# Delta-rule pairs of a hybrid two-layer trunk: causal mask in the exponent, no GpSimd products, sums of squares on column quarters, third scores ahead of the first turn

## The reference, cut to what matters

```python
q = l2norm(q) * (dk ** -0.5)
k = l2norm(k)                    # x * rsqrt(sum(x * x) + eps)
gdiff = gcum[..., :, None] - gcum[..., None, :]
decay = jnp.where(tri, jnp.exp(jnp.where(tri, gdiff, 0.0)), 0.0)
Lmat = jnp.where(strict, bc[..., :, None] * kk * decay, 0.0) + eye
sol = triangular_solve(Lmat, [v * beta, k * beta * exp(gcum)])   # u, w
qk = jnp.where(tri, einsum(qc, kc) * decay, 0.0)
q_dec = qc * jnp.exp(gcum)[..., None]
# per chunk: v_new = u - w @ state; o = q_dec @ state + qk @ v_new
#            state = state * g_last + k_dec^T @ v_new
o_a = rmsnorm(o_a, even_dn_norm) * silu(dn_gate)
```

## Time and profile before

| | |
|---|---|
| Median of 3 runs | 1393.7 us (1390.71 to 1393.97) |
| Profiled execution | 1391.1 us, span 1389.4 us |
| TensorE busy | 1334.3 us, 96% of the span |
| VectorE busy | 807.7 us, 58% |
| ScalarE busy | 576.4 us, 41% |
| GpSimd busy | 109.2 us, 8% |
| Mean granted TensorE clock | 0.98 of 2.4 GHz |

### The profile page before, as it was taken

The page is one execution under the profiler, slowest core; times in us unless marked ns, Lnnn a source line. Parts: engine busy times, 40 slices in busy tenths (PEclk is TensorE's granted clock), DMA queues, the critical chain, the costliest instruction groups (busy, mean ns, idle before and its releaser), DMA issues.

```text
span 1389.4 us, 21218 instructions
## 1 busy us (share of the span) xinstructions
PE 1334.3 (96%) x7859; PEld 1079.1 (78%) x7859; DVE 807.7 (58%) x1236; ACT 576.4 (41%) x800; POOL 109.2 (8%) x131
## 2 busy tenths in 40 slices
PE   7989989999999999999999999999999999999996
PEld 5878767777778888888888777777878888888885
DVE  4877765676656564355555655554756563455543
ACT  5522422464444442233344555554434542233342
POOL 1010010110221000000012001000310000000011
PEclk9999999999999999999999999999999999999998
DMA  8312012123345523433224322322324323433132
GB/s 256 97 33 62 16 33 61 47 61 121 92 117 157 136 81 91 113 91 104 74 79 121 106 59 76 103 75 75 91 63 116 93 68 110 124 91 91 57 94 61
DMA packets 218667, 124.95 MB, mean 90 GB/s; under 512 B 6063, under 2 KB 215450, under 8 KB 218356
## 3 DMA queue, kind: packets, MB, share of 16 engines
q1 hardware_dynamic: 213760, 112.52, 28.8%
q0 software_dynamic: 3664, 11.58, 2.9%
q10 hardware_dynamic: 1188, 0.08, 0.1%
HBM read 119.92 MB, written 9.48 MB: 93 GB/s over the span
## 4 chain that ended last, share of the span: by engine, by line
PE 87%; DVE 6%; ACT 3%; issue 2%; DMA 1%; SPq 0%; POOL 0%; DVEq 0%; ACTq 0%; POOLq 0%
PE acc L705 73%; PE acc L1159 3%; PE R L1028 2%; PE R L1042 2%; PE R L1132 1%; PE R L727 1%; DVE cta L1727 1%; PE R L837 1%; ACT wh L427 1%; PE R L884 1%; DMA xin<-in_x 1%; PE R L1091 1%; DVE wl L431 1%; DMA out<-ob 1%; DVE ml L1653 0%
## 5 line engine op out<-in xcount | busy, mean ns | idle before, releaser
L705 PE MATMUL acc<-mh,wh 128*128 128x512 f32 x1120 | 318.6, 405 | 3.2 <-ACT wh L1322 2.4
L705 PE MATMUL acc<-ml,wh 128*128 128x512 f32 x1120 | 313.0, 397 | 3.1 <-DVE ml L1653 3.1
L705 PE MATMUL acc<-mh,wl 128*128 128x512 f32 x1120 | 310.1, 396 | 1.3 <-DVE wl L1736 1.3
L431 DVE TENSOR_TENSOR wl<-raw,wh 128x2048 fp32r<-128x2048 f32 (+1 forms) x103 | 222.1, 2156 | 119.9 <-ACT wh L427 119.9
L427 ACT ACTIVATE wh<-raw 128x2048 fp32r<-128x2048 f32 (+1 forms) x111 | 200.6, 1808 | 135.6 <-PE acc L705 135.5
L705 PEld LDWEIGHTS acc<-mh,wh 128*128 128x128 f32 x1120 | 207.7, 190 | 56.2 <-issue 10.4
L705 PEld LDWEIGHTS acc<-ml,wh 128*128 128x128 f32 x1120 | 211.6, 191 | 50.8 <-DVE ml L1653 4.6
L705 PEld LDWEIGHTS acc<-mh,wl 128*128 128x128 f32 x1120 | 212.1, 191 | 47.4 <-DVE wl L1736 2.2
L2217 DVE SCALAR_TENSOR_TENSOR cta<-cb,pv,cta 128x512 f32<-128x512 f32 x88 | 66.1, 752 | 74.8 <-ACT cta L1591 68.4
L576 POOL TENSOR_TENSOR ssum<-ssum,sq 128x512 f32<-128x512 f32 x32 | 49.8, 1556 | 733.4 <-ACT sq L1272 732.7
L705 PE MATMUL acc<-ah,wl 128*128 128x512 f32 x352 | 95.4, 389 | 0.0
(11 more groups left out here) (321 smaller groups left out, 1481.9 us busy)
## 6 DMA issues: line engine op xcount, KB each, us to landing
raw<-in_ffn_w_in SPq DMA_DIRECT2D x88, 512.0 KB, 5.0
raw<-in_ffn_w_out SPq DMA_DIRECT2D x32, 384.0 KB, 4.0
raw<-in_even_w_in SPq DMA_DIRECT2D x23, 512.0 KB, 5.1
raw<-in_ffn_w_out SPq DMA_DIRECT2D x32, 320.0 KB, 3.6
raw<-in_odd_w_qkv SPq DMA_DIRECT2D x16, 512.0 KB, 4.9
rel_bias_extended<-rel_bias_rows POOLq DMA_DIRECT2D x16, 320.0 KB, 3.9
raw<-in_even_w_out SPq DMA_DIRECT2D x8, 512.0 KB, 4.8
raw<-in_odd_w_qkv SPq DMA_DIRECT2D x16, 256.0 KB, 3.1
```

What stands on the lines that cost most here:

```text
L431: nc.vector.tensor_tensor(wl[s][:, 0:n], raw[s][:, 0:n], wh[s][:, 0:n].bitcast(F32), ALU.subtract).then_inc(sem(f"w_tail{s}"), 1)
L705: last = nc.tensor.matmul(acc[2 * s + t][:, :], ws[0 if form[0] else 1][:, t, k, :], mov[0 if form[1] else 1][:, k, :], start=form == HEAD ...
```

## The change

The causal mask goes into the exponent of the transposed decay: VectorE adds a constant of 0 or -1e30 (C_CAUSAL) after the minimum with 0, so that the exponential is zero above the diagonal, and the product of qkD with the triangle is gone. The product of qd and qh moves from GpSimd to VectorE, into key_evac. token_sums uses column quarters: for each block of 128 tokens four products with 32 weight columns each, at four column positions of the array. In pair 1 the post-norm of pair 0 and the spread of q's norms come later, the transposes of v come behind Y64, key_evac and the copies of v stand elsewhere in VectorE's order, and some small buffers lie in other places. The tables of units and pieces are changed. In the attention heads the second scores come ahead of the transposes of v, in the odd pairs the third scores ahead of the first turn. Four masks are no longer in the constants.

```diff
-    put(C_M16, (row // 16 == col // 16) & (col < row))
-    for n, w in ((C_M32, 32), (C_M64, 64), (C_M128, 128)):
-        put(n, (row // w == col // w) & (row // (w // 2) > col // (w // 2)))
+    put(C_CAUSAL, np.where(row <= col, 0.0, NEG))
...
-                             ("u", "E64"), ("sqo", "A2"), ("os", "A2t")):
+                             ("u", "E64"), ("sqo", "A2"), ("os", "At")):
...
# GpSimd, dn_pair
-                for h in (0, 1):
-                    e = d[h]
-                    read(pool, ph, f"rq{h}", 0)
-                    read(pool, ph, f"grow{h}", 0)
-                    pool.tensor_tensor(e["qd"], e["qd"], e["qh"], ALU.mult).then_inc(sem(f"qd{h}"), 1)
-                for h in (0, 1):
-                    e = d[h]
-                    read(pool, ph, f"qk{h}", 0)
-                    pool.tensor_tensor(blk(e["qkD"]), blk(e["qkD"]), rows(triu), ALU.mult).then_inc(sem(f"qkD{h}"), 1)
-
             pool.wait_ge(sem("conv"), 12 * NH)
-            pool.wait_ge(sem("qkD1"), NH // 2)
+            read(pool, f"dn{NH // 2 - 1}", "qk1", 0)
...
# TensorE
                 for b in range(NB):
-                    last = nc.tensor.matmul(r[:, c0 + b:c0 + b + 1], squares[:, b * P:(b + 1) * P], ones[:, 0:1],
-                                            start=True, stop=True)
+                    for q in quarter:
+                        last = nc.tensor.matmul(r[q, c0 + b:c0 + b + 1], squares[:, b * P + q.start:b * P + q.stop],
+                                                ones[:, 0:1], start=True, stop=True, tile_position=(0, q.start))
...
                 give(fill, g[0])
+                spread(p, "rk", "sqk", "dk", p)
                 if p:
                     post_sums(p - 1)
-                spread(p, "rk", "sqk", "dk", p)
                 give(fill, g[1])
-                if p:
-                    post_rows(p - 1)
                 step(g[2], "kk", "kh", "kh", ["rk"])
-                spread(p, "rq", "sqq", "dq", p)
+                if p == 0:
+                    spread(p, "rq", "sqq", "dq", p)
...
-                g = ((4, 2, 4, 3, 3, 2, 1, 2, 2, 2, 2, 3, 2, 2), (2, 2, 2, 2, 2, 2, 1, 2, 1, 1, 1, 1, 1, 1))[p]
+                g = ((4, 2, 4, 3, 3, 2, 1, 1, 1, 1, 3, 3, 4, 3), (2, 2, 2, 2, 2, 2, 1, 2, 1, 1, 1, 1, 1, 1))[p]
                 pe.wait_ge(sem("small_U0"), p + 1)
                 tiles("c2", (0, "At", "A"), (2 * P, "A", "At"))
                 give(fill, g[0])
+                if p:
+                    post_rows(p - 1)
+                    spread(p, "rq", "sqq", "dq", p)
...
                 give(fill, g[5])
-                pe.wait_ge(sem("silu"), TURN[2 * p + 1, 2] + 1)
-                step(g[6], "vtok", "vT", None, ["ktok"])
...
                 give(fill, g[10])
+                pe.wait_ge(sem("silu"), TURN[2 * p + 1, 2] + 1)
+                step(g[6], "vtok", "vT", None, ["ktok"])
...
# diff_head
+                scores(ph, 0, 1, i)
                 values(ph, 0, UNIT["diff"] + i, vf)
-                scores(ph, 0, 1, i)
...
# odd_pair
                 values(ph, i, i + UNIT[ph], o_vf)
+                scores(ph, i, 2, i + NH)
                 turned(0)
-                scores(ph, i, 2, i + NH)
...
# ScalarE, dn_pair
-                n = ((2, 1, 0, 1, 2, 3, 1, 2), (2, 1, 0, 1, 1, 1, 1, 9))[p]
+                n = ((0, 3, 0, 0, 3, 1, 3, 2), (0, 1, 2, 0, 1, 2, 1, 9))[p]
...
# VectorE, dn_pair
-                    V.tensor_scalar(e["decT"], e["decT"], 0.0, None, ALU.min).then_inc(sem(f"dm{h}"), 1)
+                    V.scalar_tensor_tensor(out=blk(e["decT"]), in0=blk(e["decT"]), scalar=0.0, in1=rows(cblk(C_CAUSAL)),
+                                           op0=ALU.min, op1=ALU.add).then_inc(sem(f"dm{h}"), 1)
...
-                if p:
-                    post_inverse(p - 1)
+                piece("dk")
...
                 if p:
-                    post_out(p - 1)
+                    post_inverse(p - 1)
                 piece("kh")
...
                 V.tensor_tensor(eight(small["E"]), eight(small["N"]), each_eight(C_L32), ALU.mult)\
                     .then_inc(sem("small_E"), 1)
+                if p:
+                    post_out(p - 1)
...
                     V.tensor_tensor(blk(e["kd"]), blk(r[:, :]), cols(eg[h][:, 2 * NB:]), ALU.mult)
+                    read(dve, ph, f"rq{h}", 0)
+                    read(dve, ph, f"grow{h}", 0)
+                    V.tensor_tensor(e["qd"], e["qd"], e["qh"], ALU.mult).then_inc(sem(f"qd{h}"), 1)
...
                 small_update("cU1", None)
-                key_evac(0)
                 small_update("cU2", "cU1")
-                key_evac(1)
                 small_update("cU3", "cU2")
                 read(dve, ph, "cU3", 0)
                 V.transpose(small["T"], small["U"]).then_inc(sem("small_T"), 1)
-                for h in (0, 1):
-                    r = full(dve, ph, f"vtok{h}", 0)
-                    free(V.tensor_tensor(blk(d[h]["vb"]), blk(r[:, :]), cols(beta(h)), ALU.mult), ph, f"vtok{h}", 0)
+                key_evac(0)
...
                 piece("X32")
+                key_evac(1)
                 r = full(dve, ph, "Y64", 0)
                 free(V.tensor_copy(Y64, r[low, :]), ph, "Y64", 0)
+                for h in (0, 1):
+                    r = full(dve, ph, f"vtok{h}", 0)
+                    free(V.tensor_tensor(blk(d[h]["vb"]), blk(r[:, :]), cols(beta(h)), ALU.mult), ph, f"vtok{h}", 0)
...
             dn_pair(0, evacs,
-                    {"decays": 2, "kh": 1, "qh": 1, "qk": 1, "N": 2, "cU1": 1, "cU2": 1, "cU3": 1, "cX": 1, "Y32": 1, "X32": 1, "Y64": 1, "X64": 1, "vtok": 1, 0: 1, 1: 1, "o": 2})
+                    {"decays": 2, "kh": 1, "qh": 1, "qk": 1, "N": 1, "cU1": 1, "cU2": 1, "cU3": 2, "Y32": 1, "Y64": 1, "X64": 2, "vtok": 2, 0: 1, 1: 1, "o": 2})
             dn_pair(1, evacs,
-                    {"decays": 4, "kh": 1, "qh": 1, "qk": 1, "N": 2, "cU1": 1, "cU2": 1, "cU3": 1, "X32": 1, "X64": 1, 0: 1, "o": 9})
+                    {"decays": 4, "qh": 2, "qk": 1, "cU1": 1, "cU2": 1, "cU3": 2, "X32": 0, "Y64": 1, "X64": 2, 0: 1, "o": 9})
```

More of the change, by code:

```diff
@@ L60 @@
 PV_NORM = (PV_EVEN, PV_FFN, PV_ODD, PV_FFN + 8, PV_FIN)
-C_ID, C_ONE, C_TRIU, C_M16, C_M32, C_M64, C_M128, C_PERM = range(8)
-C_COS, C_SIN, C_MASK = 8 * P, 8 * P + S, 8 * P + 2 * S
-C_I32, C_L16, C_L32 = [8 * P + 3 * S + 32 * n for n in range(3)]
-C_WIDTH = 8 * P + 3 * S + 96
+C_ID, C_ONE, C_TRIU, C_CAUSAL, C_PERM = range(5)
+C_COS, C_SIN, C_MASK = 5 * P, 5 * P + S, 5 * P + 2 * S
+C_I32, C_L16, C_L32 = [5 * P + 3 * S + 32 * n for n in range(3)]
+C_WIDTH = 5 * P + 3 * S + 96
 def constants():
@@ L300, in build @@
         for n, where, at in (("A", d[0]["A"], 0), ("At", d[0]["A"], 1), ("N", d[1]["A"], 0), ("E", d[1]["A"], 1),
-                             ("A2", d[0]["A2"], 0), ("A2t", d[0]["A2"], 1), ("A4", d[0]["A2t"], 0),
-                             ("A4t", d[0]["A2t"], 1), ("A8", d[1]["A2"], 0), ("T", d[1]["A2"], 1), ("U", d[1]["A2t"], 0),
+                             ("A2", d[0]["sqk"], 0), ("A2t", d[0]["sqk"], 1), ("A4", d[0]["A2t"], 0),
+                             ("A4t", d[0]["A2t"], 1), ("A8", d[1]["sqk"], 0), ("T", d[1]["sqk"], 1), ("U", d[1]["A2t"], 0),
                              ("Y", d[1]["A2t"], 1), ("Y32", d[0]["A"], 0)):
@@ L1003, in dn_pair @@
                             pe.wait_ge(sem(f"qd{h}"), p + 1)
-                            pe.wait_ge(sem(f"qkD{h}"), p + 1)
+                            read(pe, ph, f"qk{h}", 0)
                         last = nc.tensor.matmul(o[h][:, t], vn[h][:, :], e["qkD"][:, t], start=(b == 0), stop=True)
@@ L1421, in pieces @@
                         next(evac, 0)
-                n = ((2, 1, 0, 1, 2, 3, 1, 2), (2, 1, 0, 1, 1, 1, 1, 9))[p]
+                n = ((0, 3, 0, 0, 3, 1, 3, 2), (0, 1, 2, 0, 1, 2, 1, 9))[p]
                 pieces(n[0])
-                small_out("c2", d[0]["A2"], n[1])
+                small_out("c2", d[0]["sqk"], n[1])
                 small_out("c4", d[0]["A2t"], n[2])
```

## The result

The changed kernel takes 1357.2 us (median of 4 runs) against 1392.3 us for the kernel before in the same session. One of the four, at 1476.2 us, was disturbed at a mean granted clock of 0.84 and is left out of everything that follows; the other three lie between 1356.1 and 1357.8 us, with a median of 1356.5, 35.7 us less than before. The ratio is 0.9745, 95% interval 0.9725 to 0.9765. The profiled execution took 1356.5 us (span 1354.7), 34.6 us less than that of before.

The account below looks back on a forecast made before the run. TensorE, carrying 87% of the chain, was taken as the bound. Waits -3, clock -8.5, sums -5.7 and -2.8, odd pairs -5.5 gave -25.5 on 1391.1: 1365.6 us, as runs' median 1368, range 1357 to 1380.

Parts of the forecast that it names:

- rival 1: Sums of squares: quarter loads do not overlap, 0.86 us a call; 11 of the 25.5 us lost, 1379 us; chance 0.11.
- rival 2: Delta-rule pairs: VectorE becomes the bound and TensorE's savings turn into waits; only about -11 us, 1383 us; chance 0.08.
- rival 3: Instruction stream: each of twelve sum groups stops TensorE 2.2 us, 26 us lost; 1399 us with 14 stops; chance 0.03.
- rival 4: Odd pairs: third scores gain nothing because the wait moves to scores or the next turn; 1373 us; chance 0.08.
- the clock: 50 to 250 us: five of eight low-clock pieces of 3.4 us go, 1.7 us each: -8.5 us; bounds 0 and -14.
- the sums: Sums of squares on column quarters, 0.37 us a call plus 0.2 a group: -8.5 us, 5.7 of it in 50 to 250 us.
- the odd pairs: Third scores ahead of the first turn cover TensorE's wait for ScalarE's copy of v: -5.5 us; bounds 0 and -5.6.
- the waits: TensorE's waits in 50 to 250 us fall from 16.4 to 13.3 us, so -3 us, with new waits for dk.
- The copy of c2: Delta-rule pairs: it no longer queues behind two ScalarE pieces, so 2.5 us of TensorE waiting go.
- GpSimd: Delta-rule pairs: without its products VectorE gains 2.1 us a pair and no half split takes over 1.3 us.

Follow-up runs that it names:

- the second profile: The changed kernel run once more, unchanged, beside other kernels on one chip with a second profiled execution: 1359.1 us, ratio 0.9766.
- the moves: Kernel before with only the change's orders and tables in the pairs and attention heads, without quarter sums, mask change or new odd-pair order: 1377.3 us, ratio 0.9898.

## Why the prediction was right, and where it was wrong

**The bottleneck and the direction.** TensorE was the bound, and a shorter stream, fewer waits and a higher clock were what paid. None of the rivals held: the quarters overlap (rival 1), VectorE did not cap the gain (rival 2), the stops under "issue" take 4.2 us between 50 and 250 us beside 4.3 (2.7 + 1.6) before, with 42 loads where the earlier trace rows have 39 (rival 3), and the third scores gained more than all of their wait (rival 4).

**The failed step: the clock.** I let three of eight pieces stand between 50 and 250 us and put those elsewhere at nothing, for which I had no reason: 8.5 us. In the profile one stood, and those near 391 and 1012 us went too; the one near 391 was back in the second profile. By all runs, half-clock time of the whole kernel fell from 58 to 29 us, where my five pieces are 17.

In time this was worth about 13 us. The first piece of the table lost 20.6 us; less 3.8 of waits and 7.2 of shorter sums (two groups of four, two of two and one call, at full clock), 9.6 are left, of which the large products have 8.2. That is 1.4 us for each of seven pieces and not 1.7; the 36 runs of the kernel before say the same, since there 1 us more of half-clock time goes with 0.3 us of time and not with 0.5. The two norms give 1.8 and 1.5 more (2.34 and 2.01 less 0.5 for the shorter sum). So the clock is 4.4 of the 9.1 us that I missed in the profiled execution; the sums (2.9), the odd pairs (1.7) and the waits (0.7) are the rest, and together these terms are 0.6 us too many.

The reason that I gave for single pieces was wrong as well. I had kept one for each wait that would stay, those at 88 and 173 us in the inverse of each pair among them, and both went: the trace of after has waits of 1.85, 1.94 and 1.31 us at full clock. The one that stood is the one behind pair 1's sums, which I had let go; there a wait for squares, a wait of 1.18 us for wh, and a run of one-column products come together. Nor are long one-column runs what it takes: full-width sums in the changed kernel put two pieces back behind the first sums in its one profile, but over four runs its clock is that of the changed kernel. What the runs do show is that the moves do most (58 to 39 us alone), that the parts do not add up (the moves, the quarters and the mask alone take 19, 14 and 6 us, all together 29), and that one piece of the moves, ScalarE's queue ahead of c4, costs 12 when it is put back. Why one wait brings the low level and another does not stays open.

**The odd pairs.** Forecast 5.5, measured 7.24 (7.28 alone). The term was mis-sized: the idle time in the profile begins at the modelled end of the transposes of v, so a wait behind them costs more than the row says, 0.9 us a pair instead of 0.69. In the table's fourth piece TensorE's idle time fell by 5.6 us and its busy time by 1.7, with the clock at 1.00 in both, which fits; the reading was not tested by itself.

**The sums.** Forecast 8.5. A record cost 8.5 ns, not 12, and a group 1.22 us, not 1.7: at full clock (3.49 us a group of four) the groups of four save 4.5, those of two 2.1, seven single calls 3.6 (0.37 us instead of 0.88, from start to start of what follows) and the last one 1.2, together 11.4. But what they are worth in the whole kernel is less: taking the quarters out of it cost 3 to 6 us, clock included. Behind the first group TensorE waits 1.85 us for dk, as forecast (1.9); in pair 1, where I had 2.2, it does not wait for dk, since waits for the squares and for wh, 1.8 us, came first. The Trainium skill's "TensorEngine Tiling (Array Packing)", Instruction Overhead, states some 60 cycles for every matmul. The runs had 8.5 ns between starts with the quarters in turn and 19 ns with four in a row in one quarter, both under the 25 ns that I had worked out from it. Its warning not to tile a dimension that is already small I had wrongly held against the change: the quarters divide the 128 weight columns, and the small dimension, the one moving column, stays whole. Four quarter records take 34 ns here where one full-width record takes 110.

**The waits.** Forecast 13.3, measured 12.7 us between 50 and 250 us; the total is right and the parts are not all. dk in pair 0, the wait for the first U of pair 1 (1.1, measured 1.3), rq and qk (0.9, measured 0.3 + 0.3) and the two in the first head (1.1 and 0.8, measured 1.1 and 1.0) came as written. The copy of c2 no longer makes c4 wait, priced at 2.5 us; putting the old queue back cost 6.4, so this move was worth far more than its row, because clock and stops hung on it. cX and Y32 did not wait. In their place TensorE stood for 4.2 us under "issue", of which I had written about 1.0; I put these stops down to the instruction stream, and the moved stop of the quarters alone is the evidence for it.

**GpSimd.** The split went from 5.2 to at most 1.5 us (I had written 1.3), and no L605 or L609 remains. Alone it gave 3.3 us and out of the changed kernel, by the medians, about as much. By their medians the parts alone add to 13.7 + 8.9 + 8.6 + 3.3 = 34.5 us, beside 35.7 and 32.8 in the two sessions of the changed kernel. The sum agrees, the shares do not: with the moves in, the quarters gain 3 to 6 us instead of 8.9.

## What to carry to other kernels

A wait of TensorE can have two prices: its own, and the clock that falls behind it; a row of waits shows the first alone. Try each part alone and take each out of the finished kernel: here the quarters raised the clock alone, and with the moves in they added nothing to it that the runs show. Look at the mean clock of every run before you explain pieces of one profile. And when a small product is cut into quarters of the array, let neighbouring instructions take different quarters: the order of two loops made 0.34 us of the 0.61 that a call saved here.

## What I had not expected of the hardware

- Records of 32 weight columns and one moving column start 8.5 ns apart when the quarters alternate and 19 ns apart when they do not.
- Within long runs of small tiles TensorE stops for about 2 us, at a place that depends on what came before: after 123 of 128 records of c4 in the kernel before, after 27 of cU1 with the more numerous instructions of the quarter sums ahead, after 103 of c4 in pair 1 behind a wait of 3.6 us. With the moves alone the longest such stop between 50 and 250 us is 0.6 us.
- The granted clock of a stretch can differ by three pieces of 3.4 us between kernels whose instructions are the same up to there, and over 36 runs of the kernel before the half-clock time of the whole kernel goes from 47 to 67 us.
